# A four-mixer layer on one core: attention two heads at a time, in 29 steps among projection and output tiles

## The reference

```python
def rmsnorm(x, g):
    xf = x.astype(jnp.float32)
    y = xf * lax.rsqrt(jnp.mean(xf * xf, axis=-1, keepdims=True) + EPS)
    return (y * g.astype(jnp.float32)).astype(x.dtype)

# second_block, once per layer; B = 1, S = 512, D = 1024, four mixers of width 256
mod = c_act @ w_mod[l] + b_mod[l]
sh1, sc1, gt1, sh2, sc2, gt2 = jnp.split(mod[:, None, :], 6, axis=-1)
h = rmsnorm(x, g_mix[l]) * (1.0 + sc1) + sh1
z = h @ w_in[l]                                   # 1024 x 2408
y_a = pool_mixer(parts['pool_u'], pool_w[l], pool_scale[l])   # window means over 2, 4, 8, 16 rows
y_b = chunk_band_attention(...)                   # 4 heads of 64, bias from ca_rel
y_c = dsa_attention(...)                          # 4 heads of 64, below
y_d = mla_attention(...)                          # 4 heads of 64 + 32 rotary, chunk-causal mask
mix = group_rmsnorm(jnp.concatenate([y_a, y_b, y_c, y_d], axis=-1), g_group[l])
x = x + gt1 * (mix @ w_out[l])
h = rmsnorm(x, g_ffn[l]) * (1.0 + sc2) + sh2
f = (jax.nn.silu(h @ ffn_w1[l]) * (h @ ffn_w3[l])) @ ffn_w2[l]
x = x + gt2 * f

# dsa_attention, a block of 128 queries; topk = 128
logits = jnp.einsum('bthd,bsd->bths', iqb, ik).astype(jnp.float32)    # 8 index heads
score = jnp.einsum('bth,bths->bts', iwb, jax.nn.relu(logits))
_, sel = lax.top_k(score, topk)
s = jnp.einsum('bthd,btkd->bhtk', qb, kg).astype(jnp.float32) * (Dh ** -0.5)
s = s + jnp.moveaxis(bias, -1, 1)
p = jax.nn.softmax(s, axis=-1).astype(vg.dtype)
out = jnp.einsum('bhtk,btkd->bthd', p, vg)
```

## Time and profile before

| | us |
|---|---|
| three runs | 3647.1, 3653.1, 3653.34 (median 3653.1) |
| profiled execution | 3652.87, of which the span 3651.1 |
| PE busy | 3418.3 (94%) |
| DVE, ACT, POOL busy | 1775.5 (49%), 1339.9 (37%), 1369.6 (38%) |
| first layer of kind 2: projections, latents, attention, group norm, output tiles | 127, 20, 178, 13, 47 |
| the same in the second such layer | attention 178 |

### The profile page before, as it was taken

The page is one execution under the profiler, slowest core; times in us unless marked ns, Lnnn a source line. Parts: engine busy times, 40 slices in busy tenths (PEclk is TensorE's granted clock), DMA queues, the critical chain, the costliest instruction groups (busy, mean ns, idle before and its releaser), DMA issues. The chain is left out here.

```text
span 3651.1 us, 44942 instructions
## 1 busy us (share of the span) xinstructions
PE 3418.3 (94%) x15500; PEld 2613.6 (72%) x15500; DVE 1775.5 (49%) x2772; ACT 1339.9 (37%) x2108; POOL 1369.6 (38%) x626
## 2 busy tenths in 40 slices
PE   7899999799979899997999899999999899989998
PEld 5677777588757677775887675567888664568886
DVE  5843338565447533376555337455333185363333
ACT  5755553322137555542221233233222332332221
POOL 2223334444442333334444561024445540144443
PEclk8999999899989999998999998579999995599998
DMA  3122222455421122223554222002223330012232
GB/s 120 58 69 69 69 69 89 144 187 196 137 84 58 64 75 72 72 69 110 187 201 160 92 96 75 1 18 81 98 98 104 105 110 1 1 58 96 94 103 98
DMA packets 94961, 336.36 MB, mean 92 GB/s; under 512 B 11104, under 2 KB 13792, under 8 KB 94604
## 3 DMA queue, kind: packets, MB, share of 16 engines
q1 hardware_dynamic: 94860, 335.06, 26.8%
HBM read 332.88 MB, written 8.44 MB: 93 GB/s over the span
## 5 line engine op out<-in xcount | busy, mean ns | idle before, releaser
L339 POOL TENSOR_TENSOR wLo<-wring,wHi 128x1024 fp32r<-128x1024 f32 x478 | 1173.4, 2455 | 1742.4 <-ACT wHi L319 1742.3
L363 PE MATMUL psG<-hHi,wHi 128*128 128x512 f32 x2992 | 1184.7, 396 | 35.8 <-POOL wLo L339 19.3
L363 PE MATMUL psG<-hLo,wHi 128*128 128x512 f32 x2992 | 1175.4, 393 | 8.8 <-POOL hLo L383 4.1
L363 PE MATMUL psG<-hHi,wLo 128*128 128x512 f32 x2992 | 1171.7, 392 | 0.0
L319 ACT ACTIVATE wHi<-wring 128x1024 fp32r<-128x1024 f32 x478 | 505.6, 1058 | 1013.1 <-PE psG L363 925.1
L363 PEld LDWEIGHTS psG<-hHi,wHi 128*128 128x128 f32 x2992 | 566.6, 189 | 170.1 <-issue 41.5
L363 PEld LDWEIGHTS psG<-hLo,wHi 128*128 128x128 f32 x2992 | 565.1, 189 | 144.0 <-POOL hLo L383 18.7
L363 PEld LDWEIGHTS psG<-hHi,wLo 128*128 128x128 f32 x2992 | 566.8, 189 | 116.0 <-issue 0.5
L363 PE MATMUL psG<-hidHi,wHi 128*128 128x512 f32 x704 | 276.0, 392 | 10.7 <-POOL wLo L339 10.7
L363 PE MATMUL psG<-hidHi,wLo 128*128 128x512 f32 x704 | 275.5, 391 | 0.0
L363 PE MATMUL psG<-hidLo,wHi 128*128 128x512 f32 x704 | 275.4, 391 | 0.0
(11 more groups left out here) (273 smaller groups left out, 3914.9 us busy)
## 6 DMA issues: line engine op xcount, KB each, us to landing
wring<-in_w SPq DMA_DIRECT2D x490, 512.0 KB, 3.3
modw<-in_wmod SPq DMA_DIRECT2D x96, 512.0 KB, 4.3
e_copies<-e_rows SPq DMA_DIRECT2D x2, 2048.0 KB
T_ca<-e_copies SPq DMA_DIRECT2D x2, 1792.0 KB, 7.3
T_t<-e_copies SPq DMA_DIRECT2D x2, 1792.0 KB, 11.4
...
```

The lines of the kernel that those rows point to most:

```text
L339: pool.tensor_tensor(wLo[:, c % CUTS, :, :], wring[:, c % RING, :, :], wHi[:, c % CUTS, :, :], ALU.subtract).then_inc(w_cut[c % CUTS], 1)
L363: mm = pe.matmul(psG[:, G.slot(u), :], w[:, c % CUTS, k, :], r(j), start=start and j == 0 and n == 0, stop=stop and j == len(kts) - 1 and ...
```

## The change

It touches the mixing stage of the second kind of layer alone.

- Projection: 12 tiles in front (`Z_FRONT`), the other 7 among the first attention steps (`TILE_AT`). The index scores come as two head pairs back to back at six places (`INDEX_AT`), and each of the two heads' matrices has its own slot and bank of `psS`.
- Attention: 29 steps. Step s computes the scores of pair s (two heads of one query block, stationary operands in the upper and the lower 64 rows), transposes pair s - 2 and multiplies the values of pair s - 3; then follows a tile, if the step has one. Steps 5, 6, 8 and 10 to 20 have none (step 8 has the latents' expansion). For the values, the transposed probabilities are stationary now (128x128) and 65 columns of V pass, the last a column of ones whose product is the sum for the softmax. The order of the mixers is ca, ml, sa.
- Softmax: DVE takes the minimum of the negated scores, which is ACT's bias as it stands; L1913, L1918 and L1919 go. The division and the group norm come per query block and mixer instead (`mix`, on the output as 128 queries x 256): DVE's squares, POOL's `pow` for the inverse root, ACT's scaling, PE's transposition back (`turn_mixed`), DVE's `mixed`. This takes place 16 times a layer; stage 3 goes.
- Output: the 8 output tiles with 6 of the 8 slices of the width (18 matmuls) at steps 21 to 27; the slices of sa follow in 8 short products (6 matmuls each, "rest") behind the steps, which also makes 2 more weight chunks a layer.
- Top-k: 19 rounds ahead of the steps, then 1 or 2 a step to step 21.

The diff, cut to its core (inner blocks are shown with 16 columns less of indentation):

```diff
+Z_ORDER = (2, 7, 6, 3, 4, 5, 11, 12, 13, 14, 15, 16, 0, 1, 8, 9, 10, 17, 18)
+Z_FRONT = 12
+MIXERS = ("ca", "ml", "sa")
+PAIRS = 2 * TT * len(MIXERS)
+STEPS = 29
+TILE_AT = {0: 0, 1: 1, 2: 8, 3: 9, 4: 10, 7: 17, 9: 18}
...
+OUT_AT = {21: [0], 22: [1], 23: [2], 24: [3], 25: [4], 26: [5], 27: [6, 7]}
+OUT_K = (0, 1, 2, 3, 6, 7)
+REST_K = (4, 5)
...
+INDEX_AT = {3: (0, 1), 4: (2, 3), 5: (4, 5), 6: (6, 7), 7: (8, 9), 8: (10, 11)}
...
-        units = [(kind, hd, qt) for kind in ("ml", "ca", "sa") for hd in range(HEADS) for qt in range(TT)]
...
     def index_scores(n):
-        qt, hp = idx[n]
+        hp, qt = head_pair(n)
-        pe.wait_ge(*S.is_free(s_IDX + n))
+            pe.wait_ge(*G.is_read(g[7]))
+        if qt == 1:
+            pe.wait_ge(*G.is_read(g[2 + hp]))
         for b in range(2):
-            mm = pe.matmul(psS[:, S.slot(s_IDX + n), 512 * b:512 * b + nk], iq[64 * b:64 * b + 64, hp, qt * P:(qt + 1) * P],
-                           ik[64 * b:64 * b + 64, 0:nk], start=True, stop=True)
-        mm.then_inc(S.filled(s_IDX + n), 1)
+            pe.wait_ge(*S.is_free(s_IDX + 2 * n + b))
+        for b in range(2):
+            u = s_IDX + 2 * n + b
+            pe.matmul(psS[:, S.slot(u), 0:nk], iq[64 * b:64 * b + 64, hp, qt * P:(qt + 1) * P],
+                      ik[64 * b:64 * b + 64, 0:nk], start=True, stop=True).then_inc(S.filled(u), 1)
...
+    def scores(p):
+        kind, qt, hp = pair(p)
+        nk, cols = P * (qt + 1), slice(qt * P, (qt + 1) * P)
...
+        q, k = {"ca": (caq[:, hp, cols], cak[:, hp, 0:nk]), "ml": (qn[:, hp, cols], kn[:, hp, 0:nk]),
+                "sa": (saq[:, hp, cols], sak[:, 0:nk])}[kind]
+        for b in range(2):
+            pe.wait_ge(*S.is_free(s_ATT + 2 * p + b))
+        for b in range(2):
+            u = s_ATT + 2 * p + b
+            mm = pe.matmul(psS[:, S.slot(u), 0:nk], q[64 * b:64 * b + 64, :], k[64 * b:64 * b + 64, :],
+                           start=True, stop=kind != "ml")
+            if kind != "ml":
+                mm.then_inc(S.filled(u), 1)
+        if kind == "ml":
+            for b in range(2):
+                u, r = s_ATT + 2 * p + b, 64 * b + 32 * hp
+                pe.matmul(psS[:, S.slot(u), 0:nk], qr[r:r + 32, cols], kr[r:r + 32, 0:nk], start=False, stop=True)\
+                  .then_inc(S.filled(u), 1)
...
+        if hp == 0:
+            pe.wait_ge(*O.is_free(u))
+        for hd in (2 * hp, 2 * hp + 1):
+            for c in range(qt + 1):
+                v = {"ca": Vca[:, c, hd, :], "ml": Vml[:, c, hd, :], "sa": Vsa[:, c, :]}[kind]
+                mm = pe.matmul(psO(u)[:, 65 * hd:65 * hd + 65], PT[:, (2 * p + hd % 2) % 4, c * P:(c + 1) * P], v,
+                               start=(c == 0), stop=(c == qt))
+        if hp == 1:
+            mm.then_inc(O.filled(u), 1)
...
-    def scores(n):
-        kind, hd, qt = units[n]
...
-        o = psS[:, S.slot(s), 0:nk]
-        mm = pe.matmul(o, q[b:b + 64, hd // 2, qt * P:(qt + 1) * P], k[b:b + 64, 0:nk], start=True, stop=(kind != "ml"))
-        if kind == "ml":
-            mm = pe.matmul(o, qr[32 * hd:32 * hd + 32, qt * P:(qt + 1) * P], kr[32 * hd:32 * hd + 32, 0:nk], start=False, stop=True)
-        mm.then_inc(S.filled(s), 1)
...
-        for c in range(qt + 1):
-            v = {"ca": Vca[:, hd // 2, c, b:b + 64], "ml": Vml[:, c, 64 * hd:64 * hd + 64], "sa": Vsa[:, c, 0:64]}[kind]
-            mm = pe.matmul(psG[b:b + 64, G.slot(g), qt * P:(qt + 1) * P], v, PT[:, n % 2, c * P:(c + 1) * P],
-                           start=(c == 0), stop=(c == qt))
-        if n % 8 == 7:
-            mm.then_inc(G.filled(g), 1)
-
-    for n in range(NU + 4):
-        if n < NU:
-            scores(n)
-        if 3 <= n < NU + 3:
-            turn(n - 3)
-        if n >= 4:
-            values(n - 4)
-    for j0 in (0, 2):
-        for j in (j0, j0 + 1):
-            norm_pe_quarters(pe, t_GN + j, q_GN + 2 * j, 2)
-        for j in (j0, j0 + 1):
-            norm_pe_spread(pe, t_GN + j, r_GN + j)
...
+    for s in range(STEPS):
+        if s != 8 and s < PAIRS:
+            scores(s)
+        if 2 <= s < PAIRS + 2:
+            turn(s - 2)
+        if 3 <= s < PAIRS + 3:
+            values(s - 3)
...
+        if s in TILE_AT:
+            tile(TILE_AT[s])
...
+        for name in TURN_AT.get(s, ()):
+            turn_mixed(name)
+        for j in OUT_AT.get(s, ()):
+            gemm(pe, g[f"out{j}"], CH2_WO + j, (known(hHi), known(hLo)), range(len(OUT_K)))
...
+    for qt in range(TT):
+        pe.wait_ge(*G.is_read(g["sa", qt]))
+    for j in range(KT):
+        at = 2 * (j % 4)
+        gemm(pe, g[f"rest{j}"], CH2_WR + j // 4, (tiles(hHi, REST_K[0]), tiles(hLo, REST_K[0])), (at, at + 1))
+        if j >= 1:
+            squares_of(j - 1)
+    squares_of(KT - 1)
...
+    def expo(p):
+        nk = P * (pair(p)[1] + 1)
+        for n in (2 * p, 2 * p + 1):
+            act.wait_ge(*S.is_read(s_ATT + n))
+            act.activation(Pm[:, n % 4, 0:nk], Sm[:, n % 4, 0:nk], ACT.Exp, bias=low[:, n % 4:n % 4 + 1],
+                           scale=-1.0).then_inc(p_full, 1)
...
-    def expo(n):
-        kind, hd, qt = units[n]
-        nk = P * (qt + 1)
-        act.wait_ge(nb_full, n + 1)
-        act.activation(Pm[:, n % 4, 0:nk], Sm[:, n % 2, 0:nk], ACT.Exp, bias=stat[:, n % 4, 1:2],
-                       scale=96 ** -0.5 if kind == "ml" else 1.0, accum_out=stat[:, n % 4, 2:3]).then_inc(p_full, 1)
...
+        if s - 1 in DONE_AT:
+            n = done.index(DONE_AT[s - 1])
+            y = y_of(*done[n])
+            act.wait_ge(rs_full, n + 1)
+            act.activation(y, y, ACT.Copy, scale=rs[:, n:n + 1]).then_inc(y_full, 1)
...
+        if s - 1 in TILE_AT:
+            c = CH2_Z + z_pos[TILE_AT[s - 1]] + CUTS
+            cut_rest(pool, c)
             pool.wait_ge(w_cut[c % CUTS], c // CUTS + 1)
+        for j in OUT_AT.get(s - 1, ()):
+            cut_rest(pool, CH2_WO + j + CUTS)
...
+        if first_sparse <= 2 * s + 2 < 2 * PAIRS:
+            combine(2 * s + 2)
+            combine(2 * s + 3)
+        if s in DONE_AT:
+            n = done.index(DONE_AT[s])
+            pool.wait_ge(var_full, n + 1)
+            did(pool.tensor_scalar(var[:, n:n + 1], var[:, n:n + 1], 2 * P * NORM_EPS, None, ALU.add))
+            pool.tensor_tensor(rs[:, n:n + 1], var[:, n:n + 1], half[:, :], ALU.pow).then_inc(rs_full, 1)
+            pool.wait_ge(rs_full, n + 1)
...
+    for _ in range(TAKEN_FIRST):
+        take(taken)
+        taken += 1
...
+    def mixed(name):
+        kind, qt = name
+        n, k, u = done.index(name), Y_TILE[kind], g[name]
+        dve.wait_ge(o_high, 2 * n + 2)
+        for j in range(2):
+            ins = dve.scalar_tensor_tensor(hLo[:, k + j, qt * P:(qt + 1) * P], psG[:, G.slot(u), j * P:(j + 1) * P],
+                                           gain16[:, k + j:k + j + 1], hHi[:, k + j, qt * P:(qt + 1) * P], ALU.mult, ALU.subtract)
+        ins.then_inc(G.emptied(u), 1)
...
+            dve.wait_ge(*S.is_full(u))
+            dve.tensor_tensor_reduce(Sm[:, n % 4, 0:nk], psS[:, S.slot(u), 0:nk], table, 1.0, -FILL, ALU.add, ALU.min,
+                                     low[:, n % 4:n % 4 + 1]).then_inc(S.emptied(u), 1)
...
-        dve.wait_ge(*S.is_full(u))
-        dve.tensor_tensor_reduce(Sm[:, s, 0:nk], psS[:, S.slot(u), 0:nk], table, 1.0, FILL, ALU.add, ALU.max,
-                                 stat[:, n % 4, 0:1]).then_inc(S.emptied(u), 1)
-        dve.wait_ge(*S.is_read(u))
-        dve.tensor_scalar(stat[:, n % 4, 1:2], stat[:, n % 4, 0:1], -(96 ** -0.5) if kind == "ml" else -1.0, None, ALU.mult).then_inc(nb_full, 1)
...
-    def normalise(n):
-        nk = P * (units[n][2] + 1)
-        dve.wait_ge(p_full, n + 1)
-        did(dve.reciprocal(stat[:, n % 4, 3:4], stat[:, n % 4, 2:3]))
-        dve.tensor_scalar(Pm[:, n % 4, 0:nk], Pm[:, n % 4, 0:nk], stat[:, n % 4, 3:4], None, ALU.mult).then_inc(a_full, 1)
...
+    def mix(name):
+        n, u = done.index(name), o[name]
+        y = y_of(*name)
+        dve.wait_ge(*O.is_full(u))
+        if name[0] == "pool":
+            dve.tensor_copy(y, psO(u)[:, 0:2 * P]).then_inc(O.emptied(u), 1)
+        else:
+            s = psO(u)[:, 0:65 * HEADS].rearrange("p (h d) -> p h d", h=HEADS)
+            did(dve.reciprocal(rec[:, n % 2, :].unsqueeze(2), s[:, :, 64:65]))
+            dve.tensor_tensor(y.rearrange("p (h d) -> p h d", h=HEADS), s[:, :, 0:64],
+                              rec[:, n % 2, :].unsqueeze(2).to_broadcast([P, HEADS, 64]), ALU.mult).then_inc(O.emptied(u), 1)
+        dve.wait_ge(*O.is_read(u))
+        dve.tensor_tensor_reduce(unused[:, :, :].rearrange("p a b -> p (a b)"), y, y, 1.0, 0.0, ALU.mult, ALU.add,
+                                 var[:, n:n + 1]).then_inc(var_full, 1)
...
+    for s in range(STEPS + 1):
+        for name in TURN_AT.get(s - 1, ()):
+            mixed(name)
+        for j in OUT_AT.get(s - 1, ()):
+            add_out(f"out{j}", j)
...
+        if s < PAIRS:
```

(72 more changed lines are left out.)

759 lines of the change are left out of this document (406 added, 353 removed).

## The result

The changed kernel takes 3446.3 us (median of 4 runs, 3445.0 to 3449.1) against 3653.2 for the kernel before (4 runs); the ratio is 0.9435, 95% interval 0.9419 to 0.9452. In another set of runs the same kernel took 3448.6, ratio 0.9442 (0.943 to 0.9455). The profiled execution is 3445.9, its span 3444.1.

The account below looks back on a forecast made before the run. PE was taken to set attention's length, at half clock. Five parts sum to 319 us a layer against 385, 66 less, 132 in both layers, so 3520 us from about 3653; range 3455 to 3590.

Parts of the forecast that it names:

- Steps 10 to 20, with no tile: here is the choice: Third of five parts of a layer: short attention products at the low 1.2 GHz clock, 60 us.
- gaps for hand-overs: Old attention: with short single-head products, named as what changed when the granted clock fell from 1.00 to 0.50.
- this rival: Clock stays up in steps 10 to 20: DVE's 45 us there, no later ramp, 302 a layer, 3487 us; chance 0.27.
- Changes of kind at 0.2 each: PE in attention steps: 0.2 us fixed per change of kind of product, about 40 in steps 0 to 9, 8 us.
- Transposes at 0.145: PE in attention steps: one transpose at full clock costs 0.145 us; 40 in steps 0 to 9 take 5.5.
- Values at 0.08: PE's value products, 128 stationary and 65 passing columns: 0.08 us a record, 240 records, 19 us a layer.
- Front: Until the 12th projection tile: 87 us plus 12.6 of index-score waits at six places, 99 (87 to 104).
- DVE in steps 10 to 20: DVE's load there: top-k rounds 15, minima 12, `mixed` and `mix` 17, 45 us in all.
- Stalls in steps 0 to 9: 6.5 us added to 77.5 of work, for ACT's copy and Exp and the latents' wait, giving 84.
- the split into five parts: One layer: front 99, steps 0 to 9 84, steps 10 to 20 60, steps 21 to 28 55, rest 21.
- the rival of a chain in the steps without tiles: Scores, minimum, Exp, transpose in series: 2 us more in each of 13 steps, 345 a layer, 3573 us; chance 0.13.
- the low clock: Rival: it reaches into steps 0 to 9 and 21 to 28, adding 35 us, 354 a layer, 3591 us; chance 0.10.

## Why the prediction was wrong

The step that failed is the choice in "Steps 10 to 20, with no tile: here is the choice", where I took "the low level: the stage before, of the same sort of short products, ran at 0.52". They were not of the same sort. The old ones used one half of the rows, the new ones both, and the runs with that one difference show that this decides: 0.95 over attention with the halves filled, 0.51 with the same products on the same rows, up and down again where only ml was filled. The "gaps for hand-overs" of the prediction were not the reason: PE is busy 9 of the 9 us in which the clock fell. The row that showed it lay ready: paired short products at 1.00. I gave this rival 0.27 for it and set against it "fewer hand-overs"; the difference in rows used I didn't name. In the prediction's own terms it cost 15 us a layer in steps 10 to 20 (60 instead of 45), and the 3 for a ramp in the steps behind them: 18 of the 37 that the sum was off.

The other 19 to 20 us a layer are terms of the wrong size, all of them in the rival's sum too (3487 against 3446): 3.5 in the front, 7 in steps 0 to 9, 3 in steps 10 to 20, 5 in steps 21 to 28, 1.5 in the rest. By their terms:

- **Changes of kind at 0.2 each.** This was an estimate from single-head scores of 128 and 384 columns. The starts in the changed kernel show it only at scores: 128 columns take 0.42 and 512 take 1.06, so 0.2 fixed. At the other kinds it is 0.1 or less (two transposes 0.27, six 0.71). With one such place a pair, two for ml, it is 32 places and 6.4 us a layer, where I had put 8, 11 and 6. In steps 0 to 9 and 21 to 28, where PE sets the time, that is some 11 too much.
- **Transposes at 0.145.** By the starts six take 0.71, 0.12; over 120 of them 3 us, of which 2 in the steps with tiles.
- **Values at 0.08.** Measured: 16 records 1.90 and 4 records 0.56, thus 0.112 each, 27 us a layer instead of 19; 8 too little, 4 of them in the steps with tiles. Here the price by the load of the stationary columns was right and my halving of the columns wrong, as the run with 130 passing columns shows. The Trainium skill, "TensorE: Matmul & The Clock Gate", section "LDWEIGHTS (loading the stationary operand)", has the load take P / 1.2 ns for P columns, an estimate of 107 ns for 128. The trace agrees, with 12 loads in 1.42 us, 118 ns each.
- **Front.** The six waits for relu were foreseen, at 2.1 us each; they are 1.5, 9.0 in all. With two banks these waits are gone and the whole is 19.6 us shorter, so their mechanism is shown.
- **DVE in steps 10 to 20.** 45 forecast, 39.1 measured. The prices were right: the single instructions come to 44 us (rounds 16, `mixed` 6.6, `mix` about 10, minima 11.5). But they overlap by some 5 us, which the sum had at nothing.
- **Stalls in steps 0 to 9.** 6.5 forecast; the two waits there, for the minimum and in the latents, are 2.6 and 1.6, 4.2 in all.

What held: the split into five parts and their order; DVE and PE near balance in the middle at full clock; POOL's chain for the 16 blocks on no path (no wait of PE for it in these steps); the rival of a chain in the steps without tiles is there, but at 4.3 us a layer, not 26; the low clock reached no tile step of the second kind of layer. That the range ended at 3455, since less was what "the prices above don't allow", was the same error again: the changes of kind and the transposes were priced high, and I took that sum for a floor. That the rival's 3487 came nearer than the main case owes nothing to these terms: its mechanism was right, and its sum too was 41 us too long.

The account of the 207 us, by the runs: 129 for the filled rows and the clock, and 78 for all the rest. The run with tiles in front gives 31 for their interleaving (most of which is the clock again), the next one some 6 for that of the output tiles. About 41 would remain for the halved scores, the group norm off the path and the lighter softmax, which were not separated. The first figure is from the kernel before and the two others from the changed one, so that they add up is assumed, not shown.
